# Hybrid attention and mixture-of-experts block: another order of one attention's side work among the other's units

## The reference, cut to what matters

```python
h = rmsnorm(x, norm_mix[l]);  proj = h @ w_in[l]
qa, ka, va, qb, kb, vb = jnp.split(proj, splits, axis=-1)
# A: 8 query heads on 2 key/value heads, own chunk of 64 keys and the one before, rotary, sinks
scores = einsum('bnqkgd,bnskd->bnkgqs', qc, kb) * (HEAD_DIM ** -0.5)
m = maximum(max(scores), sink);  p = exp(scores - m)
out = einsum('bnkgqs,bnskd->bnqkgd', p / (sum(p) + exp(sink - m)), vb)
# B: 8 heads, own chunk and 8 chunks before, learned bias by distance
scores = einsum('bnqhd,bnshd->bnhqs', qc, kb) * (HEAD_DIM ** -0.5) + bias
out = einsum('bnhqs,bnshd->bnqhd', softmax(scores), vb)
mixed = gates[:, :, 0] * (ya @ w_o_a) + gates[:, :, 1] * (yb @ w_o_b);  x = x + mixed @ w_out
h2 = rmsnorm(x);  x = x + hierarchical_moe(h2, ...);  return rmsnorm(x, norm_final)
```

## Time and profile before

| | |
|---|---|
| median of 3 runs | 2440.2 us |
| the profiled execution | 2440.2 us |
| its span in the trace | 2438.4 us |
| mean granted TensorE clock | 0.972 of full |
| attention stage, first to last matmul | 781.7 to 1102.2 us |

### The profile page before, as it was taken

The page is one execution under the profiler, slowest core; times in us unless marked ns, Lnnn a source line. Parts: engine busy times, 40 slices in busy tenths (PEclk is TensorE's granted clock), DMA queues, the critical chain, the costliest instruction groups (busy, mean ns, idle before and its releaser), DMA issues. The chain is left out here.

```text
span 2438.4 us, 36731 instructions
## 1 busy us (share of the span) xinstructions
PE 2290.7 (94%) x12226; PEld 1968.5 (81%) x12227; DVE 1296.3 (53%) x1939; ACT 1029.8 (42%) x1817; POOL 811.7 (33%) x782
## 2 busy tenths in 40 slices
PE   7999999999999999998999999499999999999990
PEld 6888888888887988887899998388888888888880
DVE  7112223211010888876333332877767678789885
ACT  6111112111112878874222221456556466667663
POOL 0355466540000111123222221245434444555450
PEclk9999999999999999999999999599999999999995
DMA  5356766641132776756544442699978889899987
GB/s 187 108 155 235 249 209 196 215 147 64 65 126 100 228 235 179 228 133 200 164 148 142 148 137 90 222 303 309 315 231 284 282 255 326 281 368 347 319 284 289
DMA packets 236535, 518.49 MB, mean 213 GB/s; under 512 B 24978, under 2 KB 91682, under 8 KB 235300
## 3 DMA queue, kind: packets, MB, share of 16 engines
q1 hardware_dynamic: 163060, 351.78, 41.5%
q0 software_dynamic: 30048, 86.79, 14.6%
q10 hardware_dynamic: 43344, 78.86, 9.0%
HBM read 385.64 MB, written 131.70 MB: 212 GB/s over the span
## 5 line engine op out<-in xcount | busy, mean ns | idle before, releaser
L464 DVE TENSOR_TENSOR pj_w_lo<-pj_w_raw,pj_w_hi 128x1024 fp32r<-128x1024 f32 x38 | 48.7, 1281 | 519.7 <-ACT pj_w_hi L342 519.7
L342 ACT ACTIVATE pj_w_hi<-pj_w_raw 128x1024 fp32r<-128x1024 f32 x38 | 40.2, 1059 | 529.1 <-PE pj_bank L558 477.5
L2297 POOL TENSOR_TENSOR ex_wd_lo<-weights_raw_d,ex_wd_hi 128x1024 fp32r<-128x1024 f32 x64 | 199.9, 3144 | 123.4 <-ACT ex_wd_hi L2199 119.4
L558 PE MATMUL pj_bank<-pj_hT_lo,pj_w_hi 128*128 128x512 f32 x896 | 239.5, 389 | 0.0
L558 PE MATMUL pj_bank<-pj_hT_hi,pj_w_hi 128*128 128x512 f32 x896 | 239.5, 389 | 0.0
L558 PE MATMUL pj_bank<-pj_hT_hi,pj_w_lo 128*128 128x512 f32 x896 | 239.5, 389 | 0.0
L558 PEld LDWEIGHTS pj_bank<-pj_hT_lo,pj_w_hi 128*128 128x128 f32 x896 | 168.2, 188 | 34.9
L558 PEld LDWEIGHTS pj_bank<-pj_hT_hi,pj_w_hi 128*128 128x128 f32 x896 | 168.2, 188 | 34.9
L558 PEld LDWEIGHTS pj_bank<-pj_hT_hi,pj_w_lo 128*128 128x128 f32 x896 | 168.2, 188 | 34.9
L2401 DVE TENSOR_TENSOR ex_wd_lo<-weights_raw_d,ex_wd_hi 128x1024 fp32r<-128x1024 f32 x64 | 160.2, 2542 | 3.9 <-ACT ex_wd_hi L2199 3.9
L1828 PE MATMUL mg_y_ps<-first_hi,mg_w_hi 128*128 128x256 f32 x512 | 149.1, 291 | 13.0 <-DVE mg_w_lo L1710 7.3
(11 more groups left out here) (327 smaller groups left out, 5773.3 us busy)
## 6 DMA issues: line engine op xcount, KB each, us to landing
weights_raw_g<-in_w_exp_gate_dram SPq DMA_DIRECT2D x128, 512.0 KB, 10.2
weights_raw_u<-in_w_exp_up_dram SPq DMA_DIRECT2D x128, 512.0 KB
weights_raw_d<-in_w_exp_down_dram SPq DMA_DIRECT2D x128, 512.0 KB
pj_w_raw<-in_w_feat_dram SPq DMA_DIRECT2D x38, 512.0 KB, 4.9
scratch_gates<-pj_f_hi ACTq DMA_DIRECT2D x32, 512.0 KB, 4.9
mg_g_in<-scratch_gates SPq DMA_DIRECT2D x120, 128.0 KB, 2.9
pj_x_in<-in_x_dram SPq DMA_DIRECT2D x16, 512.0 KB, 3.9
scratch_qk<-pj_f_hi ACTq DMA_DIRECT2D x16, 512.0 KB, 6.4
```

Of the source, the lines that this page charges most:

```text
L342: act.activation(w_hi[n % 2][:], w_raw[n % 2][:], ACT.Copy).then_inc(whi_done, 1)
L464: dve.tensor_tensor(w_lo[n % 2][:], w_raw[n % 2][:], w_hi[n % 2][:], ALU.subtract).then_inc(wlo_done, 1)
L558: last = pe.matmul(eight[4 * p + b][:], w[p][:, k * P:(k + 1) * P], h[:, k, b * NB:(b + 1) * NB], start=(k == 0 and n == 0), stop=(k == KD ...
L2297: pool.tensor_tensor(wd_lo[p][:, j, :], raw.buffer[2][j][:], wd_hi[p][:, j, :], ALU.subtract).then_inc(d_lo_pool, 1)
```

## The change

Three things move; no instruction of the computation is added or taken away.

1. `A_BASE`: the first step starts in unit 11 instead of 12, the last still in 126. Ten distances of 3 become nine, and most bases change between odd and even.
2. Inside a unit, ScalarE does `pt_main`, `pt_tail` and `copy_o` ahead of A's `a_exp` (slots 2 and 3) and `a_pt`; VectorE does `a_pt` behind `pt_main`, `pt_tail` and `sum_o`.
3. The value batches go two at a time: TensorE in units 3, 5, 7, 9, ScalarE and VectorE in units 4, 6, 8, 10, at VectorE as the last work of the unit.

```diff
-A_BASE = {12 + s * 114 // (A_STEPS - 1): s for s in range(A_STEPS)}
+A_BASE = {11 + s * 115 // (A_STEPS - 1): s for s in range(A_STEPS)}
@@ ScalarE
             for u in range(LAST + 1):
+                if u < B_UNITS:
+                    pt_main(u)
+                    if u % 2 == 1:
+                        pt_tail(u // 2)
+                if u % 2 == 1 and 0 <= (u - 3) // 2 < B_PAIRS:
+                    copy_o((u - 3) // 2)
                 s = a_step(u, 2)
                 if s is not None:
                     a_exp(s, (2, 3))
                 s = a_step(u, 3)
                 if s is not None:
                     a_pt(s)
-                (pt_main, pt_tail, copy_o stood here)
...
-                if 1 <= u - V_START <= V_BATCHES:
-                    a_split_v(u - V_START - 1)
+                if u > V_START and (u - V_START) % 2 == 1 and (u - V_START) // 2 * 2 < V_BATCHES:
+                    for b in range(2):
+                        a_split_v((u - V_START) // 2 * 2 + b)
@@ VectorE
                 if u + 2 < B_UNITS:
                     biased(u + 2)
-                if 2 <= u - V_START < V_BATCHES + 2:
-                    a_split_v(u - V_START - 2)
                 (a_negmax)
-                (a_pt)
                 (pt_main, pt_tail, sum_o)
+                (a_pt)
                 (a_collect, set_sinks)
+                if u > V_START and (u - V_START) % 2 == 1 and (u - V_START) // 2 * 2 < V_BATCHES:
+                    for b in range(2):
+                        a_split_v((u - V_START) // 2 * 2 + b)
@@ TensorE
-                if 0 <= u - V_START < V_BATCHES:
-                    a_turn_v(u - V_START)
+                if u >= V_START and (u - V_START) % 2 == 0 and u - V_START < V_BATCHES:
+                    for b in range(2):
+                        a_turn_v(u - V_START + b)
```

More of the change, by code:

```diff
@@ L1082, in _ @@
                     a_pt(s)
[L1083 to L1088, removed]
                 if u + 2 < B_UNITS:
@@ L1211, in _ @@
                     a_negmax(s)
-                s = a_step(u, 3)
-                if s is not None:
-                    a_pt(s)
                 if u < B_UNITS:
@@ L1220, in _ @@
                     sum_o((u - 3) // 2)
+                s = a_step(u, 3)
+                if s is not None:
+                    a_pt(s)
                 s = a_step(u, 6)
```

## The result

The changed kernel takes 2471.1 us (median of 4 runs, 2462.8 to 2473.1) against 2441.1 for the kernel before beside it: 1.0116 times as long, 95% interval 1.0102 to 1.0132. Over all 21 executions on record the changed kernel has a median of 2470.0 (2462.8 to 2473.6). Slower, as forecast. The forecast of 2463 was 8 us too low (30.0 us more, where 22.8 were forecast); 2471 is inside the range. The profiled execution took 2468.3 us, 28.1 more than the profiled one of before.

What follows compares the result with a forecast made beforehand. TensorE, busy for 94% of the span, was taken as the bound, so only its waits count. Steps 17, value pairs 6 and ends -0.2 made +22.8 us on 2440.2: forecast 2463 us, range 2444 to 2476.

Steps and rivals of the forecast that it cites:

- Part 1: VectorE in attention: A's subtraction behind B's leaves a hole empty and ends the unit later, at up to T+2.92.
- Part 3: TensorE at distances of 3: A's scores wait for A's subtraction, 0.55 us (even units) or 1.25 us (odd).
- the walk: Step-by-step sum of TensorE's waits in attention, lateness carried along: 10.8 us before, 29.6 us after, difference 18.8.
- The steps' term: Added TensorE waits over the steps of A in attention, from the new orders and table: taken as 17 us.
- the 16.5 us of old waits: TensorE's waits for VectorE between 814 and 1088 us: 14.4 for the pass over scores, 2.1 for the main subtraction.
- The last rival: TensorE's clock falls to half rate after each of four waits in the value batches: +14 us, 2477 us; chance 10%.
- Part 5: Ends of the attention stage: a gap shrinks by 0.6 us, the last step's work adds 0.4, together -0.2 us.
- Part 2: ScalarE: A's exponentials behind B's main copy free that copy, but A's transposes wait 0.6 us in odd units.
- Part 4: Value batches in pairs at the end of VectorE's even units: four TensorE waits of 1.56 us, +6 us.
- Faster: the late main copy is what counts: Rival in attention: all 16.5 us of waits go, value pairs cost 6, -10 gives 2430 us; chance 12%.
- Waits trade places: No-change rival in attention: new TensorE waits replace old ones, 16.5 for 16.5 us, about 2440 us; chance 8%.

Runs made afterwards that it cites:

- Experiments 4: Kernel before with A's copy on ScalarE and A's subtraction on VectorE moved behind B's, exponentials and table as before: 2453.8 us, ratio 1.0057.
- 5: Kernel before with A's subtraction moved behind B's on VectorE alone, ScalarE in its old order: 2454.9 us, ratio 1.0056.
- experiment 6: Kernel before with both engines' new orders (late subtraction and late exponentials), old table, value batches single: 2461.2 us against 2439.8, ratio 1.0089.
- experiment 1: Kernel before with only the value batches in pairs, last in VectorE's unit, old table and orders: 2447.6 us against 2440.3, ratio 1.0028.
- experiment 7: Kernel before with only A's exponentials of slots 2 and 3 moved behind B's copies on ScalarE: 2444.9 us, ratio 1.0014.
- 8: Kernel before with A's exponentials of slots 2 and 3 behind B's copies in odd units only: 2444.5 us, ratio 1.0021.
- experiment 9: Kernel before with A's exponentials of slots 2 and 3 behind B's copies in even units only: 2439.3 us against 2439.2, ratio 0.9997.
- experiments 2: Kernel before with value batches in pairs, but VectorE subtracting each pair one unit later, right behind its pass over the scores: 2441.2 us against 2439.2, ratio 1.0010.
- 10: Kernel before with A's collect moved from the end of VectorE's unit to right behind the pass over the scores: 2432.2 us against 2439.8, ratio 0.9973.
- experiment 12: Changed kernel with A's collect moved ahead of B's main subtraction on VectorE: 2463.7 us against 2439.2 for the kernel before, ratio 1.0097.

## Why the prediction was right, and where it was off

The parts add up: orders 21.4, pairs 7.3, table 3.2, in sum 31.9 us against 30.0 by the medians (28 by the ratio). The table's 3.2 are a wait that the changed kernel does not have; without them it is 28.7. Nothing large is left for a cause not named.

The profiled execution grew by 28.1 us where 22.8 were forecast. The clock's up to 5.1 us, which the sum had left out, are nearly all of that miss. The other terms' errors (the steps' waits +1.2, the pairs +0.8, the ends -1.5) nearly cancel, and that is luck.

- **Part 1 and Part 3 held.** The rows of unit 77 are within 0.03 us of the walk, and A's scores wait nine times. Experiments 4 and 5 show that the loss is on VectorE's queue: nothing in A's subtraction got slower, but it left a hole where VectorE idles anyway and joined the work ahead of the pass that TensorE waits for.
- **The steps' term was undersized.** I took 17, under the walk's own 18.8. The middle of experiment 6 has 19.0, its whole time 21.4. In the changed kernel the middle is 23.3 us longer (22.4, and the 0.9 that moved out); without the up to 5.1 us of the half clock at least 18.2 are left. I had rounded down because the walk missed 5.7 of the 16.5 us of old waits; that was the mistake. What it missed in the units with fewer tiles did not go away with the change: in the 28 units of the middle whose pair has fewer than four tiles to transpose, TensorE waited 3.4 us for the pass before, 4.2 in experiment 6 and 5.3 in the changed kernel.
- **The clock was left out of the sum and put in the wrong place.** The last rival had it fall in the value batches. It fell in the middle, behind waits of A's scores or B's, for up to 5 us; behind the four waits that I named it stayed at 1.00, though in experiment 1 it fell there too. The Trainium skill ("TensorE: Matmul & The Clock Gate", "HAM oscillation") has repeated waits bring the rate down; ahead of unit 126 the trace agrees in three places and not in six others with waits of 1.20 to 2.32 us. Experiment 6 bounds what hangs on it: the waits alone are enough for a slower kernel.
- **Part 5 had the right sign by luck.** At the end of the stage TensorE's waits did not shrink by 0.2 but grew by 1.3 (2.8 to 4.1 us in the rows named above). Even so that stretch is 1.7 us shorter: before, its clock of 0.79 over 16 us was worth up to 3.4 us, and after it is 1.00. Behind the stage most of that is given back, 0.63 over 14 us against 0.76. No experiment separates it.
- **Part 2's gain was none.** "This is the gain" does not hold: with part 2 alone the kernel is 4.6 us slower (7), odd units cost 5 us (8), even ones show no gain (0.9997) but can't exclude 3 us of it (9), and on top of part 1 it costs 7.9 (6). The prediction also said that VectorE's wait for the main copy would fall; with part 2 alone in even units it does (25.7), in the whole change it rises to 47.3, because part 1 empties the hole ahead of it.
- **Part 4**: 6 forecast, 7.3 measured alone, 6.8 in the changed kernel (7.7 less 0.9). I had 1.56 for each wait; they are 1.4 to 2.3 in the changed kernel. In experiment 1 the four waits sum to 6.2, the walk's own figure, and part of its 7.3 can be the clock.
- **The table was costed at nothing**, and alone costs 3 us: in its trace a wait of 2.0 in unit 11 (the first step of A meets the last value batch in one buffer) and up to 1.7 of half clock behind it. Its odd and even bases show no cost; 16 of the 32 bases changed between odd and even, half and not most. In the changed kernel no such wait stands beside that of the last pair, so it is not paid twice.
- **Rivals.** "Faster: the late main copy is what counts" falls with experiment 7, which is slower. "Waits trade places" falls with 6, which lost what the walk said, lateness carried along and all. The clock rival was half right, as above.

## What to carry to other kernels

On an engine that runs in order, side work is free in the hole where the engine waits for its next input, and can cost up to its length as the last work ahead of what the bound engine waits for. The same subtraction or copy of 0.60 us costs next to nothing or much by its place in the queue (experiments 2, 5 and 10): 32 subtractions, 19 us of work, cost 15 us at the end of their units, and taking the 32 collects out of that place gave back 7.6. Look for the holes in the timeline of the engines that are not the bound, and count what stands between the end of the hole and the next thing that the bound engine needs. With TensorE 96% busy in the stretch (94% of the span), reordering one copy on VectorE still gave 7.6 us.

## What the runs showed of the hardware that was not expected

- Waits of TensorE of 1.25 to 1.68 us were followed by stretches partly at 1.2 GHz (means of 0.57 to 0.66) in three places of one execution, and waits of 1.20 to 2.32 us in six others by none. The wait of 2.32 us in unit 9 was followed by such a stretch in experiment 12 and not in the changed kernel. A trace shows one draw; a kernel with such waits should be timed often.
- The output copy can wait for the store of the pair four before, which leaves from the same one of four buffers: 2.34 us in the row of experiment 9, none in the changed kernel.
